# Deep transformer stack in one kernel: norms by column halves, a three-step root, one conditioning product and the side loads moved

## The chip, the cores and the metric

The kernel runs on one core of one Trainium2 chip. The metric is device time in microseconds (us) of one execution, as the median of several; less is better.

## What is computed

Two residual stacks, one after the other, all in 32-bit floats, with 256 tokens of width 1024. The first has two layers, each with four layer norms; the second has two layers with root-mean-square norms that are modulated by a conditioning vector, and mixtures of 16 experts. Cut to what matters here:

```python
for i in range(2):                                   # first block
    x = layer_norm(a * x + 0.5 * swiglu_ffn(x, ...), ...)            # FFN 0, FFN 2
    h = diff_attention(x) if i == 0 else pool_mixer(x)
    x = layer_norm(a * x + h, ...)                                   # mix_norm
    x = layer_norm(a * x + memory_cross_attention(x, mem, ...), ...) # xa_norm
    x = layer_norm(a * x + 0.5 * swiglu_ffn(x, ...), ...)            # FFN 1, FFN 3
for layer in range(2):                               # second block, lat = x
    mod_l = split(silu(c) @ ada_w[layer] + ada_b[layer], 6)          # and mod_c for the context
    h_l = rms_norm(lat, norm1_w) * (1 + mod_l[1]) + mod_l[0]
    y_l = hyena_mixer(h_l) if layer == 0 else sliding_window_attention(h_c, h_l)
    lat = lat + mod_l[2] * y_l
    h_l = rms_norm(lat, norm2_w) * (1 + mod_l[4]) + mod_l[3]
    lat = lat + mod_l[5] * expert_choice_ffn(h_l, ...)               # layer 0: the context too
return rms_norm(lat, final_norm_w)
```

## The kernel before

It is written out by hand, one instruction stream for each engine, with semaphores between them. The 256 tokens are NT = 2 tiles of 128 partitions; in the second block the context adds two more (tiles 2 and 3). A class `Plan` counts, in the order of the work, how many ring loads, work tiles, norms and parameter rows each stage uses, and every engine waits for counts worked out from it, so the order in the plan, in SP's loads and in TensorE's products has to be the same.

**The ring.** All weights pass through 12 slots of 1 MB (`ring`), loaded by SP in order. `load` (L707) waits until the slot's last user is done (`loads_used`). In the stages that use split weights (the four FFNs, the attention projections and outputs of the first block) a weight takes two slots, one for the value and one for its high part: VectorE or ScalarE rounds it, VectorE subtracts (`split_load` L2184, and L2191 and L2193 in the trace; `weight_low` L2200), and TensorE makes three products in place of one. `split_first` makes the first splits of an FFN early: in `cross_attention(1)` of VectorE (L2472) it stands behind ctx_norm and ahead of xa_norm1, and splits the first load of FFN 3.

**Work tiles and accumulators.** `work` is four banks that are used in turn; TensorE's `open_tile` waits until the bank's last content has been read. `acc` is four banks for one product of 256 x 1024: two column halves for each of two tiles.

**Norms.** `layer_norm` (L2290) waits for the tile's product, adds it to the rows (L2300), takes statistics (L2306), waits for ScalarE's square root, refines its reciprocal in five small steps (`newton_root` L2216), and writes the rows (L2319). It takes a gain row (L2312) and a bias row from `prow`. `mod_norm` (L2330) is the modulated one; `add_product` (L2660) adds the scaled product ahead of it. TensorE then turns the rows to columns (`normed_to_cols`, transposes, L875), and ScalarE copies them to SBUF (L1746 or, where it makes high parts, L1763).

**Parameter rows.** POOL loads gains, biases and modulation rows in a fixed order into the five slots of `prow` (L3029), each when an older row has been given back (`give_back`, L2396). Rows 14 to 16 belong to ctx_norm, rows 17 and 18 are the gain and bias of xa_norm1.

**Conditioning products.** `ada(q)`, q from 0 to 5, is 8 loads of 1 MB and 32 products of a 128 x 32 weight with 512 columns. ScalarE copies the result (`ada_out`), and POOL's `store_mods(q)` adds the bias (L3041), stores four rows to memory (L3045), waits for them and loads the next bias (L3033). ada(2) is done between values(1,1) and cross_attention(1), behind which stand ctx_norm, xa_norm1 and FFN 3. On TensorE, from L1654:

```python
            memory_values(1, 1)
            ada(2)
            cross_attention(1)
            normed_to_cols("ctx_norm", rows_h)
            normed_to_cols("xa_norm1", read=False)
            ffn(3)
```

On SP, L796 to L799, the loads are in the same order. On POOL, L3079 to L3088: rows up to 13, `store_mods(2)`, rows 14 to 16, then, once the last attention tile has been read, the load of the context, then rows 17 and on.

**Start.** ScalarE's queue loads the constants and x; POOL's queue, once x has landed (L3053 to L3064): mem (1 MB), three hyena tables, the router's weights, small vectors, the first conditioning bias, a mask and the first four parameter rows.

**First expert norm.** `moe_norm0` works on four tiles: lat (0, 1), whose product is hy_out0, and context (2, 3), whose product is hy_out1. For each pair VectorE mixes both tiles and then norms both. TensorE turns tiles 0 and 1 within hy_out1, then runs ada(3), then turns tiles 2 and 3. The loads of ada(3) are followed in the ring by those of expert 0.

Of the kernel before, what the change touches and what calls it, by code (L numbers as in the profile page):

```python
# [40 lines left out]
P = 128  # L41
# [191 lines left out]
def make_plan():  # L233
# [216 lines left out]
def build_program(nc, io, out, mod_rows, x_rows):  # L450
    plan = make_plan()
    with ExitStack() as ctx:
# [34 lines left out]
        head_tmp = sb("head_tmp", [P, NT * DA_H])  # L487
# [218 lines left out]
        def _(sp):  # L706
# [89 lines left out]
            load_values(1, 1)  # L796
            load_ada(2)
            load_cross_attention(1)
# [54 lines left out]
        def _(pe):  # L853
# [60 lines left out]
            def tile_to_acc(stage, n, x, j, last, blocks=range(KB)):  # L914
# [4 lines left out]
                for cb in range(2):  # L919
                    for half in range(2):  # L920
                        landed(n + 2 * cb + half)
                        w = slot(n + 2 * cb + half, 4)
                        for k in range(4):
                            kk = 4 * half + k
                            if kk not in blocks:
# [3 lines left out]
                               acc_full if fin and cb == 1 else None, done=int(last and k == 3))  # L929
# [66 lines left out]
            def out_product_split(stage, x_stage):  # L996
# [4 lines left out]
                for j in range(NT):  # L1001
# [3 lines left out]
                    for cb in range(2):  # L1005
                        for wp, xp in SPLIT_ORDER:
# [5 lines left out]
                            for half in range(2):  # L1012
# [6 lines left out]
                                for k in range(4):  # L1019
# [3 lines left out]
                                       kk == 0 and not wp and not xp, fin, acc_full if fin and cb == 1 else None,  # L1023
# [20 lines left out]
            def ffn(i):  # L1044
# [9 lines left out]
                def down(u, n, first_tile, tmore, smore, last=False):  # L1054
# [9 lines left out]
                    for h, j in order:  # L1064
                        for half in range(2):
                            final = last and h == 1 and half == 1
                            b, c = (2 * u + h) % 4, slice(half * 512, half * 512 + 512)
                            mm_split(acc[:, 2 * j + half, :],
                                     (gated_high[:, b, j * P:(j + 1) * P], gated_low[:, b, j * P:(j + 1) * P]),
                                     (high[:, h, c], low[:, h, c]), u == 0 and h == 0, last and h == 1,  # L1070
                                     acc_full if final else None, done=2 * int(h == 1 and j == NT - 1 and half == 1))
# [546 lines left out]
            pe.wait_ge(hy_landed, 16 * 3)  # L1618
            t = plan["hy_mlp1"].tiles
# [27 lines left out]
            for j in range(NT):  # L1647
                for g in range(4):
                    for a in range(2):
                        fin = g == 3 and a == 1  # L1650
                        mm(acc[:, 2 * j + g // 2, (g % 2) * 256:(g % 2) * 256 + 256],
                           pooled[:, 2 * g + a, j * P:(j + 1) * P], w[:, 2 * g + a, :], a == 0, a == 1,
                           acc_full if fin else None, done=int(fin and j == NT - 1))
# [84 lines left out]
        def _(act):  # L1738
# [241 lines left out]
            nc.scalar.activation(head_sq[:, 1, :], head_sq[:, 0, :], ACT.Sqrt).then_inc(root_ready, 1)  # L1980
# [38 lines left out]
            ada_out(2)  # L2019
# [112 lines left out]
            for s in range(2):  # L2132

                for i in range(NT * s, NT * (s + 1)):
                    norm_root("moe_norm0", i, i)
                if s:
                    ada_out(3)
                for i in range(NT * s, NT * (s + 1)):
                    cols_from_rows(col_tile("moe_norm0", i, 0), i * P)
# [25 lines left out]
        def _(dve):  # L2165
# [50 lines left out]
            def newton_root(v, s, r, tmp):  # L2216
# [975 lines left out]
```

## Time and profile before

| | |
|---|---|
| time, median of 3 runs | 2728.52 us (2727.0 to 2732.47) |
| the profiled execution's own time | 2730.94 us |
| its span, first to last instruction | 2728.9 us |
| TensorE (PE) busy | 2488.3 us, 91% |
| VectorE (DVE) busy | 1454.5 us, 53% |
| ScalarE (ACT) busy | 497.9 us, 18% |
| GpSimd (POOL) busy | 122.1 us, 4% |
| mean granted clock of TensorE | 0.96 |
| moved by DMA | 712.30 MB, mean 261 GB/s |

The page divides the span into 40 slices of 68 us. TensorE is busy for nine tenths or more in nearly all of them up to slice 30; the GB/s are between 58 and 280 up to slice 22 and about 422 in the two expert stages, where the chain that ended last runs through the loads ring<-in_moe_up and ring<-in_moe_down. PE is TensorE's matmul, PEld its weight load. A row of the timeline gives start, length, engine, source line, operation, output<-input, and in brackets how long the engine was idle before and what it waited for. SPq, ACTq and POOLq are DMA issues.

### The profile page before, as it was taken

The numbers are of one execution on the slowest core, as the hardware profiler recorded it, in microseconds if no ns is written. First come the engines' busy times: TensorE is split into PE (matmuls) and PEld (weight loads), VectorE is DVE, ScalarE is ACT, GpSimd is POOL, SyncE is SP. The second block draws the span as 40 slices with busy tenths as digits, with TensorE's granted clock in tenths as the row PEclk, the third lists the DMA queues.
The fourth block names the chain that finished last, engine by engine and source line by source line (L and its number), as shares of the span: only waits on it lengthen the run. The fifth ranks groups of instructions, "written<-read, shape, count | busy, mean of one in ns | idle before, by whom it ended". The sixth has DMA issues, their size and how long they took to land. (4 is left out here: it accounts for less than half of the span.)

```text
span 2728.9 us, 37076 instructions
## 1 busy us (share of the span) xinstructions
PE 2488.3 (91%) x14566; PEld 1708.9 (63%) x14566; DVE 1454.5 (53%) x2390; ACT 497.9 (18%) x942; POOL 122.1 (4%) x134
## 2 busy tenths in 40 slices
PE   7999999999999998998999799999999987777777
PEld 6997777999899588997676333333334863333333
DVE  6768554876876568767888623222234442112113
ACT  0004424100100131003331111111110631111111
POOL 1000000000000000003221100000000000000000
PEclk9999999999999998998999889999999998888898
DMA  7557642555556655561224899999996437999997
GB/s 252 185 215 280 245 147 93 182 185 200 170 186 212 251 172 179 185 204 58 62 62 162 336 398 422 422 422 422 422 420 263 171 115 324 422 422 422 422 422 308
DMA packets 234146, 712.30 MB, mean 261 GB/s; under 512 B 12645, under 2 KB 134517, under 8 KB 178624
## 3 DMA queue, kind: packets, MB, share of 16 engines
q1 hardware_dynamic: 223328, 676.37, 64.4%
q0 software_dynamic: 9856, 32.16, 3.3%
q10 hardware_dynamic: 864, 2.40, 0.2%
q8 instruction: 68, 1.11, 0.2%
q14 instruction: 30, 0.25, 0.0%
HBM read 708.69 MB, written 2.20 MB: 261 GB/s over the span
## 5 line engine op out<-in xcount | busy, mean ns | idle before, releaser
L859 PE MATMUL work<-ring,scratch 128*64 128x512 f32 (+1 forms) x3008 | 551.7, 636 | 107.6 <-DMA ring<-in_moe_up 69.8
L859 PE MATMUL work<-rows_h_parts,ring_parts 128*128 128x256 f32 x3072 | 550.5, 285 | 20.0 <-DVE ring_parts L2193 10.6
L859 PEld LDWEIGHTS work<-rows_h_parts,ring_parts 128*128 128x128 f32 x3072 | 477.1, 194 | 24.5 <-issue 10.3
L859 PEld LDWEIGHTS work<-ring,scratch 128*64 128x64 f32 (+1 forms) x3008 | 145.9, 126 | 489.0 <-issue 283.4
L859 PE MATMUL work<-cols_x_parts,ring_parts 128*128 128x256 f32 x1536 | 414.3, 285 | 0.0
L2193 DVE TENSOR_TENSOR ring_parts<-ring,ring_parts 128x2048 fp32r<-128x2048 f32 x132 | 302.6, 2292 | 4.5
L859 PEld LDWEIGHTS work<-cols_x_parts,ring_parts 128*128 128x128 f32 x1536 | 287.2, 194 | 1.5
L859 PE MATMUL acc<-ring_parts,rows_h_parts 128*128 128x512 f32 x896 | 264.3, 391 | 0.0
L2751 DVE COPY scratch<-work 128x512 f32<-128x512 f32 x32 | 22.1, 692 | 367.6 <-PE work L859 367.6
L859 PE MATMUL work<-scratch 128*128 128x256 f32 (+4 forms) x1040 | 198.8, 379 | 6.5 <-issue 4.2
L859 PEld LDWEIGHTS acc<-ring_parts,rows_h_parts 128*128 128x128 f32 x896 | 165.1, 188 | 33.2 <-issue 1.0
L2191 DVE CAST ring_parts<-ring 128x2048 fp32r<-128x2048 f32 x132 | 161.2, 1221 | 44.3 <-DMA ring<-in_ffn_w_in 36.0
L859 PEld LDWEIGHTS work<-scratch 128*128 128x128 f32 (+1 forms) x1040 | 151.8, 194 | 26.3 <-issue 12.4
L1785 ACT ACTIVATE scratch<-work 128x256 f32<-128x256 f32 x88 | 33.8, 384 | 674.4 <-PE work L859 674.4
L2761 DVE TENSOR_TENSOR scratch<-work,scratch 128x512 f32<-128x512 f32 x32 | 22.1, 692 | 229.9 <-PE work L859 229.9
L859 PE MATMUL acc<-ring_parts,scratch_parts 128*128 128x512 f32 x352 | 136.9, 389 | 0.0
L1889 ACT ACTIVATE scratch<-work 128x512 f32<-128x512 f32 x64 | 38.2, 597 | 496.9 <-PE work L875 275.7
L859 PE MATMUL work<-ring,cols_x 128*128 128x512 f32 x256 | 113.4, 604 | 1.9 <-ACT cols_x L1746 1.9
L2244 DVE TENSOR_TENSOR scratch<-scratch,work 128x256 f32<-128x256 f32 x88 | 37.0, 420 | 146.1 <-ACT scratch L1785 146.1
L2767 DVE TENSOR_TENSOR rows_x<-rows_x,work 128x512 f32<-128x512 f32 x128 | 83.7, 685 | 56.2 <-PE work L859 56.2
L859 PEld LDWEIGHTS work<-ring,cols_x 128*128 128x128 f32 x256 | 49.4, 194 | 63.2 <-issue 63.0
L1746 ACT ACTIVATE scratch<-work 128x512 f32<-128x512 f32 (+3 forms) x118 | 59.9, 524 | 156.9 <-PE work L859 110.2
(309 smaller groups left out, 2934.6 us busy)
## 6 DMA issues: line engine op xcount, KB each, us to landing
ring<-in_moe_down SPq DMA_DIRECT2D x128, 1024.0 KB, 25.9
ring<-in_moe_up SPq DMA_DIRECT2D x127, 1024.0 KB, 26.4
ring<-in_moe_gate SPq DMA_DIRECT2D x121, 1024.0 KB, 25.1
ring<-in_ffn_w_in SPq DMA_DIRECT2D x88, 1024.0 KB, 6.6
ring<-in_ada_w SPq DMA_DIRECT2D x48, 1024.0 KB, 11.6
ring<-in_ffn_w_out SPq DMA_DIRECT2D x44, 1024.0 KB, 6.3
ring<-in_xa_wkv SPq DMA_DIRECT2D x16, 1024.0 KB, 6.8
ring<-in_da_w_qkv SPq DMA_DIRECT2D x12, 1024.0 KB, 6.5
```

The source lines that it names most:

```text
L859: ins = nc.tensor.matmul(o, lhsT, rhs, start=start, stop=stop, **kw)
L1746: nc.scalar.activation(dst, src, ACT.Copy).then_inc(tile_read[t % 4], 1)
L1785: nc.scalar.activation(silu_buf[:, (2 * what[0] + what[1]) % 4, :], work[:, t % 4, 0:S], ACT.Silu).then_inc(silu_ready, 1)
L1889: nc.scalar.activation(dst, src, ACT.Copy).then_inc(tile_read[(t + q) % 4], 1)
L2191: nc.vector.tensor_copy(high, w).then_inc(arrived, 16)
L2193: nc.vector.tensor_tensor(low, w, high.bitcast(F32), ALU.subtract).then_inc(split_ready, 1)
L2244: step(nc.vector.tensor_tensor(g, silu_buf[:, m % 4, :], work[:, t % 4, S:2 * S], ALU.mult))
L2751: nc.vector.tensor_copy(up_part, work[:, b % 4, :]).then_inc(tile_read[b % 4], 1)
L2761: nc.vector.tensor_tensor(down_part, work[:, b % 4, :], out_gate, ALU.mult).then_inc(tile_read[b % 4], 1)
L2767: nc.vector.tensor_tensor(there, there, work[:, b % 4, :], ALU.add).then_inc(tile_read[b % 4], 1)
```

## The change

- **Side loads.** On POOL five small tables come first (positions, the two lambda vectors, the sub-norm gain, the sink). Then POOL waits for the sixth SiLU of FFN 0 before it loads mem, the hyena tables, the router, the bias, the mask and the rows.
- **Halves.** TensorE signals `acc_full` for each column half; the last FFN step goes half by half. `layer_norm` adds and takes statistics by halves, `add_product` multiplies and adds by halves.
- **Root.** ScalarE takes the root of four times the variance; VectorE needs three steps, not five. The head norm of the first attention has as many steps as before.
- **Conditioning product ada(2)** goes from ahead of mix_norm1 to between ctx_norm and xa_norm1, with its loads and its store.
- **First expert norm.** The context tiles are mixed and normed one after the other; TensorE runs ada(3) between turning tile 2 and tile 3.

```diff
-    norm("mix_norm1", before=[values(1, 1), ada(2)])
+    norm("mix_norm1", before=[values(1, 1)])
     cross_attention(1)
     norm("ctx_norm")
-    norm("xa_norm1")
+    norm("xa_norm1", before=[ada(2)])
...
-        if j == NT:
+        if j == NT + 1:
             ada(3)()
...
             load_values(1, 1)
+            load_cross_attention(1)
             load_ada(2)
-            load_cross_attention(1)
             ffn(3)
...
-                                       kk == 0 and not wp and not xp, fin, acc_full if fin and cb == 1 else None,
+                                       kk == 0 and not wp and not xp, fin, acc_full if fin else None,
...
-                    order = [(h, j) for h in range(2) for j in range(NT)]
+                    order = [(h, j, half) for h in range(2) for j in range(NT) for half in range(2)]
                     if last:
-                        order = [(h, j) for j in range(NT) for h in range(2)]
+                        order = [(h, j, half) for j in range(NT) for half in range(2) for h in range(2)]
...
             memory_values(1, 1)
-            ada(2)
             cross_attention(1)
             normed_to_cols("ctx_norm", rows_h)
+            ada(2)
             normed_to_cols("xa_norm1", read=False)
             ffn(3)
...
+            normed_to_cols("moe_norm0", rows_h, tiles=[NT], read=False)
             ada(3)
-            normed_to_cols("moe_norm0", rows_h, tiles=range(NT, 2 * NT))
+            normed_to_cols("moe_norm0", rows_h, tiles=[NT + 1])
+            for piece in range(2):
+                read_out(pe, col_tile("moe_norm0", NT, piece))
...
-                nc.scalar.activation(root[:, i:i + 1], spread[:, i:i + 1], ACT.Sqrt).then_inc(root_ready, 1)
+                nc.scalar.activation(root[:, i:i + 1], spread[:, i:i + 1], ACT.Sqrt, scale=-1.0).then_inc(root_ready, 1)
...
             memory_values(1, 1)
-            ada_out(2)
             cross_attention(1)
             for j in range(NT):
                 norm_root("ctx_norm", j, NT + j)
             norm_root("xa_norm1", 0, 0)
             for j in range(NT):
                 cols_from_rows(col_tile("ctx_norm", j, 0), (NT + j) * P)
-            split_cols("xa_norm1", 0)
+            ada_out(2)
             norm_root("xa_norm1", 1, 1)
-            split_cols("xa_norm1", 1)
+            for j in range(NT):
+                split_cols("xa_norm1", j)
...
-                step(nc.vector.reciprocal(r, s))
-                step.settle()
-                step(nc.vector.tensor_tensor(tmp, r, r, ALU.mult))
-                step.settle()
-                step(nc.vector.tensor_tensor(tmp, tmp, v, ALU.mult))
-                step.settle()
-                step(nc.vector.tensor_scalar(tmp, tmp, -0.5, 1.5, ALU.mult, ALU.add))
-                step.settle()
-                step(nc.vector.tensor_tensor(r, r, tmp, ALU.mult))
+            def newton_root(minus_four, half, r):
+
+
+                step(nc.vector.reciprocal(half, half))
+                step.settle()
+                step(nc.vector.scalar_tensor_tensor(out=r, in0=half, scalar=half, in1=minus_four, op0=ALU.mult, op1=ALU.mult))
+                step.settle()
+                step(nc.vector.scalar_tensor_tensor(out=r, in0=r, scalar=3.0, in1=half, op0=ALU.add, op1=ALU.mult))
                 step.settle()
...
                     for h in range(2):
-                        step(nc.vector.bn_stats(stats[:, j, h, :], rows_x[:, j, h * 512:(h + 1) * 512]))
+                        half = rows_x[:, j, h * 512:(h + 1) * 512]
+                        if prepare is None:
+
+                            dve.wait_ge(acc_full, 2 * (NT * use + j) + h + 1)
+                            ins = nc.vector.scalar_tensor_tensor(out=half, in0=half, scalar=x_scale, in1=acc[:, 2 * j + h, :],
+                                                                 op0=ALU.mult, op1=ALU.add)
+                            if h:
+                                ins.then_inc(acc_read, 1)
+                                dve.wait_ge(acc_read, NT * use + j + 1)
+                            else:
+                                step(ins)
+                                step.settle()
+                        step(nc.vector.bn_stats(stats[:, j, h, :], half))
...
                     if not last:
-
+                        if free is not None and i >= NT:
+                            dve.wait_ge(acc_full, 2 * NT * (plan[free].acc + 1))
                         step(nc.vector.tensor_tensor(h, x, factor, ALU.mult))
...
-                    if out_bias:
+                    mix_first = out_bias and s != streams[-1]
+                    if mix_first:
 
                         for i in mine:
                             mix(i, scale)
                         give_back(2)
                     for i in mine:
-                        if mix is not None and not out_bias:
+                        if mix is not None and not mix_first:
                             mix(i, scale)
...
+            pool.wait_ge(silu_ready, plan["ffn0"].silu + 2 * FFN_HEAD)
             pool.dma_start(rows_x[:, NT:2 * NT, :], io["mem"][0].rearrange("(j p) d -> p j d", p=P)).then_inc(mem_landed, 16)
...
             before_ctx = 8 * DEPTH - 2
-            rows_until(before_ctx)
-            store_mods(2)
             rows_until(before_ctx + 3)
 
             at = plan["xa_att1"]
             read_out(pool, at.tiles + attention_order(NT * XA_H)["o", NT * XA_H - 1])
             pool.dma_start(rows_x[:, NT:2 * NT, :], io["ctx"][0].rearrange("(j p) d -> p j d", p=P)).then_inc(ctx_landed, 16)
-
-
+            store_mods(2)
             rows_until(before_ctx + 10)
```

## Rows read from the trace of the kernel before

**Rows 1.** The page: busy time of the engines; GB/s in 40 slices of 68 us.
```profile
PE 2488.3 (91%) x14566; PEld 1708.9 (63%) x14566; DVE 1454.5 (53%) x2390; ACT 497.9 (18%) x942; POOL 122.1 (4%) x134
...
GB/s 252 185 215 280 245 147 93 182 185 200 170 186 212 251 172 179 185 204 58 62 62 162 336 398 422 422 422 422 422 420 263 171 115 324 422 422 422 422 422 308
```

**Rows 2.** Waits, 0 to 80 us: us in total, times, longest.
```profile
PE work L859 <- DVE ring_parts L2193: 9.4, 3, 7.5
```

**Rows 3.** Timeline, VectorE's fourth weight split: start, us.
```profile
36.19 1.23 DVE L2191 CAST ring_parts<-ring 128x2048 fp32r<-128x2048 f32 x1 [5.99 <-DMA ring<-in_ffn_w_in]
```

**Rows 4.** Windows: length, busy by engine, granted clock, DMA share, GB/s.
```profile
39.80:44.00 4.20, 4.20 (x19) 4.20 (x20) 4.10 (x5) 0.00 (x0) 0.00 (x0) 0.50 0.95 344
...
48.00:52.00 4.00, 4.00 (x30) 3.74 (x29) 3.90 (x5) 0.39 (x1) 0.00 (x0) 1.00 0.02 4
```

**Rows 5.** DMA queues, 0 to 100 us: POOL's queue, packets, MB, share.
```profile
q0 software_dynamic: 1344, 4.27, 12.9%
```

**Rows 6.** Timeline, ffn_norm0: add, statistics, root's first step, output, TensorE's wait.
```profile
211.81 1.28 DVE L2300 SCALAR_TENSOR_TENSOR rows_x<-rows_x,acc 128x512 f32<-128x512 f32 x2 [2.93 <-PE acc L859]
213.13 1.29 DVE L2306 BATCH_NORM_STATS2 stats<-rows_x 128x6 f32<-128x512 f32 x2
...
215.96 0.16 DVE L2218 RECIPROCAL rstd<-root 128x1 f32<-128x1 f32 x1
...
216.92 1.28 DVE L2319 SCALAR_TENSOR_TENSOR rows_x<-rows_x,rstd,prow 128x1024 f32<-128x1024 f32 x1
...
226.53 2.13 PE L875 MATMUL work<-consts,rows_x 128*128 128x128 f32 x16 [3.14 <-DVE cols_x_parts L2213]
```

**Rows 7.** Timeline, ada(2): its products, ScalarE's copy, the next parameter row.
```profile
942.26 7.07 PE L859 MATMUL work<-ring,act_col 128*32 128x512 f32 x64
...
949.46 0.60 ACT L1746 ACTIVATE ada_raw<-work 128x512 f32<-128x512 f32 x1 [6.50 <-PE work L859]
...
958.93 0.54 POOL L3029 DMA_DIRECT2D prow<-in_norm_w  x1
```

**Rows 8.** Timeline around ctx_norm and xa_norm1.
```profile
997.75 0.55 POOL L3029 DMA_DIRECT2D prow<-in_ln_g  x1 [0.33 <-issue]
...
1013.21 1.27 SPq L719 DMA_DIRECT2D ring<-in_ffn_w_in  x2
...
1016.64 1.23 DVE L2191 CAST ring_parts<-ring 128x2048 fp32r<-128x2048 f32 x1
...
1019.37 1.91 PE L875 MATMUL work<-consts,rows_h 128*128 128x128 f32 x16
...
1020.12 1.28 DVE L2300 SCALAR_TENSOR_TENSOR rows_x<-rows_x,acc 128x512 f32<-128x512 f32 x2
...
1023.29 2.04 ACT L1746 ACTIVATE cols_x<-work 128x512 f32<-128x512 f32 x4
...
1032.98 1.97 PE L875 MATMUL work<-consts,rows_x 128*128 128x128 f32 x8 [4.29 <-DVE rows_x L2319]
```

**Rows 9.** Timeline, eight products of ada(4) after a wait.
```profile
2044.69 1.94 PE L859 MATMUL work<-ring,act_col 128*32 128x512 f32 x8 [1.42 <-DMA ring<-in_ada_w]
```

**Rows 10.** DMA issues, 706 to 709 us: a parameter row, KB, us to landing.
```profile
prow<-in_pool_scale POOLq DMA_DIRECT2D x1, 512.0 KB, 4.3
```

**Rows 11.** Timeline, the last tile of mod_norm0 turned.
```profile
1247.30 1.97 PE L875 MATMUL work<-consts,rows_h 128*128 128x128 f32 x8 [3.57 <-DVE rows_h L2357]
```

**Rows 12.** Timeline: ada(3), last tile of moe_norm0; the window of the DMA gap.
```profile
1540.21 5.36 PE L859 MATMUL work<-ring,act_col 128*32 128x512 f32 x48
...
1554.56 1.97 PE L875 MATMUL work<-consts,rows_h 128*128 128x128 f32 x8 [5.03 <-DVE rows_h L2357]
...
1582.00:1584.00 2.00, 2.00 (x8) 0.64 (x6) 0.00 (x0) 0.00 (x0) 0.00 (x0) 0.57 0.46 70
```

**Rows 13.** Timeline: the last tile of moe_norm1 turned; the program's last output rows.
```profile
2246.83 1.97 PE L875 MATMUL work<-consts,scratch 128*128 128x128 f32 x8 [7.00 <-DVE scratch L2357]
...
2724.57 1.28 DVE L2354 SCALAR_TENSOR_TENSOR rows_h<-rows_x,rstd,prow 128x1024 f32<-128x1024 f32 x1
```

More of the change, by code:

```diff
@@ L928, in tile_to_acc @@
                             mm(acc[:, 2 * j + cb, :], x(kk, j), w[:, k, :], kk == 0, fin,
-                               acc_full if fin and cb == 1 else None, done=int(last and k == 3))
+                               acc_full if fin else None, done=int(last and k == 3))
             def split_done(stage, k):
@@ L1060, in down @@
                     high, low = parts(n, 2)
-                    order = [(h, j) for h in range(2) for j in range(NT)]
+                    order = [(h, j, half) for h in range(2) for j in range(NT) for half in range(2)]
                     if last:
-                        order = [(h, j) for j in range(NT) for h in range(2)]
[L1064 to L1071, printed above, removed]
+                        order = [(h, j, half) for j in range(NT) for half in range(2) for h in range(2)]
+                    for h, j, half in order:
+                        final = last and h == 1
+                        b, c = (2 * u + h) % 4, slice(half * 512, half * 512 + 512)
+                        mm_split(acc[:, 2 * j + half, :],
+                                 (gated_high[:, b, j * P:(j + 1) * P], gated_low[:, b, j * P:(j + 1) * P]),
+                                 (high[:, h, c], low[:, h, c]), u == 0 and h == 0, final,
+                                 acc_full if final else None, done=2 * int(h == 1 and j == NT - 1 and half == 1))
                 def run(events, tb, lb, it, tper, lper):
@@ L2131, in _ @@
                     hyena_highs(c + 2, 0)
[L2132 to L2139, printed above, removed]
+            for i in range(NT):
+                norm_root("moe_norm0", i, i)
+            for i in range(NT):
+                cols_from_rows(col_tile("moe_norm0", i, 0), i * P)
+            norm_root("moe_norm0", NT, NT)
+            cols_from_rows(col_tile("moe_norm0", NT, 0), NT * P)
+            norm_root("moe_norm0", NT + 1, NT + 1)
+            ada_out(3)
+            cols_from_rows(col_tile("moe_norm0", NT + 1, 0), (NT + 1) * P)
             experts(0)
@@ L2327, in tile_root, with mod_norm @@
                 c = slice(i, i + 1)
-                newton_root(spread[:, c], root[:, c], rstd[:, c], newton[:, c])
-            def mod_norm(stage, streams, mix=None, out_bias=False, last=False, dst=lambda i: rows_h[:, i, :]):
+                newton_root(spread[:, c], root[:, c], rstd[:, c])
+            def mod_norm(stage, streams, mix=None, out_bias=False, last=False, dst=lambda i: rows_h[:, i, :], free=None):
                 at = plan[stage]
@@ L2390, in mod_norm @@
                         norm_tile(i, factor, shift)
-                    give_back(2 * int(not last) + 1 + int(mix is not None and not out_bias))
+                    give_back(2 * int(not last) + 1 + int(mix is not None and not mix_first) * (1 + int(out_bias)))
             def give_back(rows):
@@ L2663, in mix @@
                     at, j = plan[name(i // NT)], i % NT
[L2664 removed]
                     step.settle()
[L2666 to L2669 removed]
+                    for h in range(2):
+                        c = slice(h * 512, h * 512 + 512)
+                        dve.wait_ge(acc_full, 2 * (NT * at.acc + j) + h + 1)
+                        ins = nc.vector.tensor_tensor(mix_tmp[:, c], acc[:, 2 * j + h, :], scale[:, c], ALU.mult)
+                        if h:
+                            ins.then_inc(acc_read, 1)
+                            dve.wait_ge(acc_read, NT * at.acc + j + 1)
+                        else:
+                            step(ins)
+                            step.settle()
+                        step(nc.vector.tensor_tensor(rows_x[:, i, c], rows_x[:, i, c], mix_tmp[:, c], ALU.add))
                     step.settle()
@@ L2943, in _ @@
             dve.wait_ge(x_back, 32)
[L2944 removed]
+            mod_norm("moe_norm0", [0, 1], mix=add_product(lambda s: f"hy_out{s}"), out_bias=True, free="hy_out1",
                      dst=lambda i: h_main[:, i, :] if i < NT else rows_h[:, i, :])
```

60 lines of the change are left out of this document (27 added, 33 removed).

## The prediction

> **What bounds the kernel now.** I read the page first. TensorE is busy for 91% of the span, and the line of GB/s is flat at about 422 in slices 24 to 30 and 34 to 38 [rows 1]. So there are two kinds of stage: up to slice 22 TensorE sets the pace and an edit is worth what it takes out of TensorE's idle time; in the two expert stages the transfers do, and an edit is worth what it moves the point from which they run without a gap. Next I read what TensorE waited for in the first 80 us, then the timeline of each norm that the diff touches, and for each moved step the timelines of SP and POOL, whose queues run in order.
>
> **Start of the kernel.** TensorE loses 9.4 us to weight splits, 7.5 of them at once [rows 2]. VectorE makes these splits and was itself waiting for the load that it splits, 6.0 us at 36.19 [rows 3]. Then TensorE runs at 0.50 of its clock, that is at 1.2 of its 2.4 GHz, from 39.80 to 44.00 [rows 4]. In the same time POOL's queue moves 4.27 MB [rows 5]: mem, tables and parameter rows. The change lets all but the five small ones wait for the sixth SiLU of the first FFN. Removed: the two later stalls, 8.8 us, and half of 4.2 us at the low clock, 2.1; together 11.0 us (bounds 8 and 12). The first stall, 0.6, is VectorE's own and stays. The delayed transfers then land beside FFN 0; cover for them is there, since the DMA engines move only 4 GB/s in 48 to 52 while TensorE is busy all the time [rows 4]. Cost 0.
>
> The Trainium skill, "DMA: Bandwidth & Descriptors", section "Issuing engines are not separate DMA queues", speaks against this edit: transfers issued by any engine share the same 16 DMA engines and interleave. By it the bytes are only moved and can delay ring loads later; by the row of 48 to 52 there is idle time to take them. The first would make the sum some 10 us longer, and that is one of the rivals below.
>
> **Halves and the three-step root.** Each norm tile has five small steps of the root, from 215.96 to 216.92, 0.96 us, so 0.19 each [rows 6]; two less save 0.385 per tile. Where VectorE waits for the accumulator, as at 211.81 [rows 6], the first half (0.64 for the add, 0.65 for its statistics [rows 6]) can be done before the second half of the product is there: 1.25 us, once per norm, less 0.04 for a settle in each tile. The variance still takes two steps, so nothing there. What counts is whether TensorE waits:
> - ffn_norm0: TensorE waits 3.14 us at 226.53 for VectorE [rows 6]. 1.25 + 2 x 0.385 - 0.05 = 2.0 gained (at most 3.1).
> - mix_norm0, xa_norm0, ffn_norm1, ffn_norm2: in none did I find TensorE waiting for the rows; key and value products lie over them. 0, and if that cover were gone 0.8 to 2.0 each to be had.
> - mod_norm0 with ffn_norm3 ahead of it: four tiles in a chain, TensorE waits 3.57 us for the last [rows 11]. 1.25 + 4 x 0.385 - 0.1 = 2.7 gained.
> - moe_norm1: TensorE waits 7.00 us [rows 13]; the add and statistics of the first half lie under the product, the root is shorter: 2.0 gained, and the expert stage starts that much earlier.
> - mod_norm1 0.4 and last_norm 2 x 0.385 = 0.8 (VectorE's chain ends the program, last tile at 2724.57 [rows 13]).
> The head norm of the first attention has as many steps as before: 0.
>
> **First expert norm tile by tile.** Tile 2 is now normed before tile 3 is mixed, but its output may be written only once hy_out1 is done, so it comes some 3.5 us after 1540.21, and only then does TensorE run ada(3), which before began at 1540.21 [rows 12]. TensorE turns the last tile some 2 us sooner than 1554.56 [rows 12]. But the loads of expert 0 wait in the ring for ada(3)'s slots, and from there on the DMA engines are all but saturated until their one gap around 1582 (0.46 of their share in 1582 to 1584 [rows 12]). Starting them 4 to 5 us later fills that gap and then costs something; the two mixes by halves add 0.8 before. I take 1.0 lost, between 2.5 gained and 4 lost.
>
> **Conditioning product ada(2).** Here the sign is decided. Removed: 7.0 us of TensorE at 942.26 [rows 7], bare, since the mix norm needs only values(1,1) as cover (its second tile is ready then). So everything up to xa_norm1 is 7.0 earlier. All times below are the old ones less 7.0. Three queues are passed:
> 1. SP. The eight ada(2) loads now stand behind xa_out1 and ahead of ffn(3). Ring of 12 slots: the last four ada(2) loads need the first four slots of xa_out1, freed where SP issued at 1013.21 [rows 8], now 1006.2; the first load of ffn(3) needs the fifth of them, freed as the second block of the last tile ends (1011.6), and queues behind four ada loads. Five loads of 1 MB at about 2.5 us (422 GB/s [rows 1]) plus 2 for the start: it lands at 1021.3. Before, it had landed long ago, and VectorE split it at 1016.64 with no wait [rows 8]. VectorE's order is ctx_norm, this split, xa_norm1. It comes to the split at 1008.9 (two roots shorter) and waits 12.4 us. Split 3.5 (1016.64 to 1020.12), so xa_norm1 starts at 1024.8.
> 2. ScalarE reads the ctx tiles only after the root of xa_norm1's tile 0, 3.2 us after that norm starts (1020.12 to 1023.29 [rows 8]): 1028.0, and for 2.0 us. TensorE, done with the ctx turns at 1014.4 (the time of [rows 8] less 7.0), waits for these reads. ada(2) starts at 1030.1. After so long an idle time it starts at the low clock, where eight of its products take 1.94 us [rows 9] instead of 0.88 (7.07/8 [rows 7]): about 2 more, so it ends at 1039.2.
> 3. POOL. store_mods(2) now stands behind the ctx load and ahead of the parameter rows 17 and 18. Those are ln_g and ln_b of xa_norm1, which went out right behind the ctx load at 997.75 [rows 8]. Row 17 now needs ScalarE's copy of ada(2), the sum, four stores, their landing, and the bias load: 9.5 us from 949.46 to 958.93 [rows 7]. So it goes out at 1048.8 and lands 4.3 to 7 us later (4.3 with little else in flight [rows 10]; I take 4.5, as the ring is full by then): 1053.3. VectorE stands in xa_norm1's tile 0 with the variance done, waiting for the gain row. Then 1.28 + 0.58 + 1.28: tile 0 at 1056.5; tile 1 is 6.1 later (6.4 before, from 1020.12 and 1032.98), 1062.6.
> TensorE turned that tile at 1032.98 [rows 8]. So 29.6 us are lost here, with the 7.0 already credited; bounds 25 and 34, from the landings (4.3 to 7; 5 loads at 2.5 to 3) and the low clock.
>
> **Sum.** -11.0 - 2.0 + 29.6 - 2.7 + 1.0 - 0.4 - 2.0 - 0.8 = +11.7. The profiled execution took 2730.94 us (span 2728.9), the median is 2728.52; the sum gives 2742.6 against the first and 2740.2 against the second. I predict 2740.2.
>
> **Rivals.**
> - The change does what it is meant to do: neither row nor load is late. For it speaks that the bare waits for xa_norm1 and TensorE's 7.0 us are real; against it the order of two queues. Tile 1 is then turned at 1025.9, 36.7 us better: 2703.5.
> - Only the ring load is late, the row is in time (if rows 17 and 18 went out before the store). Tile 1 at 1040.3: 2717.9.
> - Only the row is late, the load in time: ada(2) ends at 1025.3, row at 1039.4, tile 1 at 1048.6: 2726.2, no change that counts.
> - Slower still: the 4.1 MB of side loads meet the ring loads of FFN 0 and delay a split beyond its lead. It decides from the point where a ring load lands more than one FFN half later than now; the price is the DMA time of these bytes, 4.1 MB at 400 GB/s, 10 us, and all the start gained is given back: 2750.
>
> **How the numbers follow.** Forecast 0.62, with a range of its own of 2734 to 2746 from the bounds at the start, at xa_norm1 and at the expert stage. Slower still 0.09, row only 0.08, load only 0.08, neither 0.08, between these 0.05. About 0.2%, 5.5 us, is what a measurement of this kernel tells from no change. Faster by more: neither, load only and a little: 0.18. Within: row only and the forecast's tail: 0.11. Slower: 0.71. For 8 in 10 I take in row only and slower still: 2725 to 2751.
>
> **What the new profile would show.** No split stall of TensorE near 40 us, and the second FFN step about 11 us sooner. In the waits: VectorE idle 10 to 14 us for ring<-in_ffn_w_in just before xa_norm1 and about 24 us for the ln_g row inside its first tile, TensorE idle some 15 us before ada(2) and again after it. mix_norm1 is followed at once by the turns. ada(3) starts about 5 us after hy_out1, and the DMA gap near 1582 is gone. The prediction is wrong if the ln_g row does not wait for the store of ada(2), or if ffn(3)'s first load comes before ada(2)'s.

## The result, and the profile after

The changed kernel takes 2743.72 us (median of 4 runs, 2742.9 to 2746.08) against 2727.76 us for the kernel before; the ratio is 1.0053 (95% interval 1.0041 to 1.0065), so it is slower by 11 to 18 us. The prediction was 2740.2 us, 11.7 more than before. The profiled execution has a span of 2743.4 us against 2728.9: 14.5 more.

The page after: busy time of the engines, and GB/s in 40 slices, to be read against [rows 1].

```profile
PE 2486.0 (91%) x14566; PEld 1698.2 (62%) x14566; DVE 1449.1 (53%) x2337; ACT 497.3 (18%) x942; POOL 123.3 (4%) x134
...
GB/s 244 237 236 292 178 146 111 193 184 211 157 184 243 140 172 162 185 206 100 62 62 161 265 419 422 422 422 422 422 422 291 170 92 328 422 422 422 422 422 312
```

The work of the engines has hardly changed: TensorE has 2.3 us less, VectorE 5.4 less, POOL 1.2 more. The time is in waits, and the waits of 1000 to 1070 us say which (us in total, times, longest):

```profile
DVE rows_x L2320 <- DMA prow<-in_ln_g: 28.4, 1, 28.4
...
PE work L874 <- DVE rows_x L2325: 24.0, 2, 19.7
...
PE work L858 <- ACT cols_x L1748: 16.7, 1, 16.7
...
DVE ring_parts L2194 <- DMA ring<-in_ffn_w_in: 12.7, 1, 12.7
```

In the kernel before, the same stretch has no wait for a row or for a load. The timeline shows the waits of the changed kernel in their order (start, us, engine, line; in brackets the idle time before it and what ended it):

```profile
998.52 25.05 SPq L718 DMA_DIRECT2D ring<-in_ffn_w_in  x4
...
1008.63 1.23 DVE L2194 CAST ring_parts<-ring 128x2048 fp32r<-128x2048 f32 x1 [12.74 <-DMA ring<-in_ffn_w_in]
...
1012.10 0.68 DVE L2303 SCALAR_TENSOR_TENSOR rows_x<-rows_x,acc 128x512 f32<-128x512 f32 x1
...
1015.40 2.04 ACT L1748 ACTIVATE cols_x<-work 128x512 f32<-128x512 f32 x4
1017.80 9.65 PE L858 MATMUL work<-ring,act_col 128*32 128x512 f32 x64 [16.66 <-ACT cols_x L1748]
...
1027.57 0.60 ACT L1748 ACTIVATE ada_raw<-work 128x512 f32<-128x512 f32 x1 [10.13 <-PE work L858]
...
1036.94 0.54 POOL L3051 DMA_DIRECT2D prow<-in_ln_g  x1 [0.49 <-issue]
...
1043.68 1.28 DVE L2320 SCALAR_TENSOR_TENSOR rows_x<-rows_x,mean_var,prow 128x1024 f32<-128x1024 f32 x1 [28.43 <-DMA prow<-in_ln_g]
...
1053.40 1.97 PE L874 MATMUL work<-consts,rows_x 128*128 128x128 f32 x8 [4.26 <-DVE rows_x L2325]
```

The reader sees one chain through five engines. VectorE comes out of ctx_norm at 995.9 and stands 12.7 us in front of the split of a load that SP could issue only behind the eight of ada(2). Its statistics of xa_norm1 come late by that, ScalarE's root and reads of the ctx tiles behind them, TensorE's ada(2) behind those, ScalarE's copy behind ada(2), POOL's store behind the copy, and the row ln_g behind the store. For that row VectorE stands another 28.4 us inside tile 0. In [rows 8] the same split ran with no wait and the last tile was turned at 1032.98.

How far the changed kernel is from the one before at the same instruction, from both timelines:

| TensorE at | before | after | difference | step |
|---|---|---|---|---|
| first turn of ffn_norm0 | 221.43 | 210.75 | -10.7 | start -10.7 |
| its last turn | 226.53 | 213.28 | -13.3 | ffn_norm0 -2.6 |
| last turn of xa_norm1 | 1032.98 | 1053.40 | +20.4 | ada(2) +33.7 |
| last turn of mod_norm0 | 1247.30 | 1265.11 | +17.8 | -2.6 |
| last turn of mod_norm1 | 2054.09 | 2069.81 | +15.7 | moe_norm0, experts 0, mod_norm1 -2.1 |
| last turn of moe_norm1 | 2246.83 | 2261.27 | +14.4 | -1.3 |
| VectorE's last output row | 2724.57 | 2739.03 | +14.5 | last norm 0.0 |

### The profile page after: what moved, and what is told of

Its sections match the earlier page's. It is cut to its first block and busy times, and to the rows that moved or that the text cites. A ratio compares the mean times of both kernels' runs of the same rounds, so it can differ in the third digit from the quotient of the medians.

```text
span 2743.4 us, 37025 instructions
## 1 busy us (share of the span) xinstructions
PE 2486.0 (91%) x14566; PEld 1698.2 (62%) x14566; DVE 1449.1 (53%) x2337; ACT 497.3 (18%) x942; POOL 123.3 (4%) x134
## 5 line engine op out<-in xcount | busy, mean ns | idle before, releaser
L858 PE MATMUL work<-ring,scratch 128*64 128x512 f32 (+1 forms) x3008 | 557.5, 642 | 111.1 <-DMA ring<-in_moe_up 69.9
L858 PEld LDWEIGHTS work<-rows_h_parts,ring_parts 128*128 128x128 f32 x3072 | 475.2, 193 | 15.9 <-issue 9.9
L858 PEld LDWEIGHTS work<-scratch 128*128 128x128 f32 (+1 forms) x1040 | 148.6, 191 | 25.1 <-issue 12.4
```

The source lines that it names most:

```text
L858: ins = nc.tensor.matmul(o, lhsT, rhs, start=start, stop=stop, **kw)
```

## The experiments

Each was timed beside the kernel before. The last column is the ratio's distance from 1 times 2730 us; its interval is about 2.5 to 4 us to either side. Times at an instruction are from the one profiled execution of each kernel, and such an execution can lie 2 us or more from the median.

| run | median us | ratio to before (95%) | us against before |
|---|---|---|---|
| changed kernel | 2743.72 | 1.0053 (1.0041 to 1.0065) | +14.5 |
| row_first | 2720.27 | 0.9961 (0.9947 to 0.9974) | -10.6 |
| split_behind | 2729.06 | 0.9995 (0.9986 to 1.0004) | -1.4 |
| both_moved | 2704.80 | 0.9902 (0.9887 to 0.9917) | -26.8 |
| ada_back | 2710.84 | 0.9928 (0.9914 to 0.9941) | -19.7 |
| only_ada | 2761.49 | 1.0114 (1.0099 to 1.0129) | +31.1 |
| only_start | 2719.02 | 0.9960 (0.9947 to 0.9972) | -10.9 |
| only_math | 2719.34 | 0.9962 (0.9949 to 0.9975) | -10.4 |
| ctx_reads_first | 2732.24 | 1.0012 (1.0003 to 1.0021) | +3.3 |
| copy_first | 2730.76 | 1.0002 (0.9993 to 1.0010) | +0.5 |
| moe_back | 2741.47 | 1.0046 (1.0034 to 1.0058) | +12.6 |
| both_root | 2701.97 | 0.9895 (0.9881 to 0.9909) | -28.7 |
| both_root_moe_back | 2703.24 | 0.9904 (0.9890 to 0.9918) | -26.2 |

**Is the whole loss in the move of ada(2)?** The move undone on all five queues, the rest kept (ada_back), and the move alone on the kernel before (only_ada). The edit of ada_back on the plan, SP and POOL; TensorE's and ScalarE's parts go back in the same way:

```diff
-    norm("mix_norm1", before=[values(1, 1)])
+    norm("mix_norm1", before=[values(1, 1), ada(2)])
...
-    norm("xa_norm1", before=[ada(2)])
+    norm("xa_norm1")
...
-            load_cross_attention(1)
             load_ada(2)
+            load_cross_attention(1)
...
-            rows_until(before_ctx + 3)
+            rows_until(before_ctx)
+            store_mods(2)
+            rows_until(before_ctx + 3)
```

> The changed kernel with the conditioning product ada(2) put back to its old place on all five queues, its loads and store_mods(2) with it; all else as changed. Theory (the whole loss is in this move, net of the 7.1 us that it takes from the mix norm): the second tile of xa_norm1 is turned 13.2 us earlier than in the kernel before, 33.7 earlier than in the changed kernel, so 33 us less than the changed kernel, about 19 less than the kernel before. Rival (a part of the loss comes from the side loads, which now meet the ring loads of the first FFN, or from the norms' new order): clearly less than 33, below 25.

> The kernel before with one part of the change alone: the conditioning product ada(2) moved to xa_norm1, on SP, TensorE, ScalarE and POOL. Theory: the whole loss of the change is here; the product's 7.1 us at the mix norm are gained and about 40.5 are lost at xa_norm1, so 33 us more than the kernel before. Rival (the loss needs the other parts, which make everything ahead of xa_norm1 earlier and so the ring load relatively later): 25 or less.

ada_back is at -19.7 us, so 34.2 less than the changed kernel; only_ada is at +31.1. Both are what the theory gave (-19 and +33), and both are beyond the 25 at which the rivals began, only_ada's interval too (27 to 35). What the change loses, it loses by this move. Only_ada's waits of 1000 to 1070 us show the same two late transfers with none of the other edits in the kernel:

```profile
DVE rows_x L2314 <- DMA prow<-in_ln_g: 27.0, 1, 27.0
...
PE work L859 <- ACT cols_x L1746: 16.6, 1, 16.6
...
DVE ring_parts L2191 <- DMA ring<-in_ffn_w_in: 12.3, 1, 12.3
```

**Which of the two comes last?** Row_first repairs the row alone, split_behind the load alone, both_moved both.

```diff
+            rows_until(before_ctx + 5)
             store_mods(2)
             rows_until(before_ctx + 10)
```

```diff
-                split_first(2 * i + 1, 1)
+                if i == 0:
+                    split_first(2 * i + 1, 1)
                 layer_norm(f"xa_norm{i}", f"xa_out{i}", ALPHA, LN_EPS)
```

> The changed kernel with one step of POOL's queue moved: the parameter rows 17 and 18 (ln_g and ln_b of xa_norm1) go out right behind the ctx load and ahead of store_mods(2), as they did before the change. Theory (two late things, of which the row comes last): the rows land near 1005 us, long before they are wanted; VectorE still begins xa_norm1 at 1012.1, since the load of ffn(3) is as late as ever; ada(2) still runs from 1017.8 to 1027.5 and is now what comes last. The second tile is turned near 1029.5 instead of 1053.4: 24 us less than the changed kernel, about 9.5 less than the kernel before. Rival 1 (the row is late for another cause, such as its slot in the ring of rows): no change. Rival 2 (only the ring load decides): no change, and only the split's place helps.

> The changed kernel with VectorE's split of the first load of ffn(3) taken from ahead of xa_norm1 and made behind it; POOL's queue stays as changed. Theory: xa_norm1 begins at once behind ctx_norm, at 995.9 instead of 1012.1, so ScalarE reads the ctx tiles 16 us earlier and ada(2) runs from about 1002 to 1011.5; the row still waits for the store behind it (9.5 us) and its landing (6.7), is there near 1027.5 instead of 1043.7, and the second tile is turned near 1037: 16 us less than the changed kernel, so about 1.5 less than the kernel before. Rival (the ring load itself is what ada(2) or the row waits for): the late load then holds the same things as before, and no more than 4 us are gained.

> Both repairs at once: rows 17 and 18 ahead of store_mods(2), and the split of ffn(3)'s first load behind xa_norm1; ada(2) stays under the norm, where the change put it. Theory: nothing of xa_norm1 waits for a transfer; its second tile is done near 1008.6, ada(2) ends near 1011.5, the late load lands near 1008.6 and is split by 1012, and ffn(3) begins about 40 us earlier than in the changed kernel (1056.1): about 40 us less than the changed kernel, 25 less than the kernel before. Rival (the two waits hide a third of the same length, such as the second load of ffn(3), which queues behind the same transfers): 5 to 15 us of this stay in new waits of TensorE for splits at the start of ffn(3).

Against the changed kernel they gain 25.1, 15.9 and 41.3 us, where 24, 16 and 40 were expected. Each rival falls: the row is held by the store and nothing else, and the load matters although the row comes last, because ada(2), on which the row waits, hangs on it. The timeline of row_first shows the load as late as ever and ada(2) 0.5 us later, with no wait for a row; the tile is now turned at 1031.8, not at the 1029.5 expected, since VectorE waits 5.70 us for a root that stands behind the copy of ada(2):

```profile
1009.17 1.23 DVE L2194 CAST ring_parts<-ring 128x2048 fp32r<-128x2048 f32 x1 [12.87 <-DMA ring<-in_ffn_w_in]
...
1018.34 9.73 PE L858 MATMUL work<-ring,act_col 128*32 128x512 f32 x64 [16.78 <-ACT cols_x L1748]
...
1031.79 1.09 PE L874 MATMUL work<-consts,rows_x 128*128 128x128 f32 x8 [2.69 <-DVE rows_x L2325]
```

So at the tile row_first is 21.6 us ahead of the changed kernel, where 24 was expected. Another 3.3 us come between mod_norm0 and mod_norm1, a stretch that varies from run to run (see below); that the medians give 25.1 is in part luck.

In split_behind ada(2) starts 15 us sooner and at full clock, and the row is still the last thing to come:

```profile
1002.69 7.07 PE L858 MATMUL work<-ring,act_col 128*32 128x512 f32 x64 [1.15 <-ACT cols_x L1748]
...
1020.25 0.54 POOL L3052 DMA_DIRECT2D prow<-in_ln_g  x1 [0.49 <-issue]
1026.48 1.28 DVE L2320 SCALAR_TENSOR_TENSOR rows_x<-rows_x,mean_var,prow 128x1024 f32<-128x1024 f32 x1 [26.96 <-DMA prow<-in_ln_g]
```

**Is it one chain or two losses?** If it is one chain, the load must be to be had off it without touching the split. The reads of the ctx tiles go ahead of the root of tile 0 (ctx_reads_first), and then the copy of ada(2) too (copy_first):

```diff
-            norm_root("xa_norm1", 0, 0)
             for j in range(NT):
                 cols_from_rows(col_tile("ctx_norm", j, 0), (NT + j) * P)
             ada_out(2)
+            norm_root("xa_norm1", 0, 0)
```

That is copy_first; in ctx_reads_first the root stands between the reads and ada_out(2).

> The changed kernel with one step of ScalarE moved: its reads of the ctx tiles stand ahead of the root of xa_norm1's first tile instead of behind it. The late load and the late row stay. Theory (the chain to the row runs load, split, statistics, root, ctx reads, ada(2), store, row; this takes ada(2) off the load): ada(2) runs from about 1002 instead of 1017.8, the row is there near 1027.5 instead of 1043.7, and 16 us are gained against the changed kernel, as much as by the split behind the norm, although xa_norm1 itself still begins at 1012. Rival (the load and the row are two separate losses that add up): the row's part stays, under 5 gained.

> The last edit on ScalarE one instruction further: the ctx reads and also its copy of ada(2) stand ahead of the root of xa_norm1's first tile. In the run before, ada(2) itself ran from 1002.8 to 1009.9, but its copy waited until 1015.9 behind that root, which waits for the late split. Theory: the copy is made at 1010, the row goes out near 1020 instead of 1025.9 and is there near 1026.5; 5 us less than that run, 16 to 17 less than the changed kernel, 1.5 to 2 less than the kernel before. Rival (the copy is not what POOL's queue waits for): no gain over that run.

Ctx_reads_first gains 11.2 us against the changed kernel, not 16. The expectation had overlooked the copy: ada(2) was done at 1009.9, but its copy stood in ScalarE's queue behind a root that waits for the late split.

```profile
1002.80 7.07 PE L858 MATMUL work<-ring,act_col 128*32 128x512 f32 x64 [1.15 <-ACT cols_x L1748]
...
1015.79 0.20 ACT L1799 ACTIVATE root<-spread 128x1 f32<-128x1 f32 x1 [13.36 <-DVE spread L2315]
1015.90 0.58 ACT L1748 ACTIVATE ada_raw<-work 128x512 f32<-128x512 f32 x1
```

With the copy ahead as well, it is made at 1008.73, the row goes out at 1021.11 instead of 1025.86, and xa_norm1's last tile is turned at 1036.99, 16.4 us sooner than in the changed kernel. The medians give 14.0 us, with an interval that holds both 14 and 16. It is one chain: the late load costs time through the row. That the gains of the two repairs add up all the same (25.1 and 15.9 against 41.3 together) is no contradiction, as each repair takes one link out of a series.

**What is left between the two repairs and more?** In both_moved VectorE waited 3.65 us for a root that stood behind the copy of ada(2). The split behind the norm has a price too, which the theory of both_moved left out and its rival put at 5 to 15 us: it stands ahead of VectorE's split columns of the last tile (L2216), for which TensorE now waits:

```profile
PE work L858 <- DVE cols_x_parts L2216: 3.6, 1, 3.6
```

ffn(3) starts 4.69 us after the last turn in both_moved and in split_behind, and 2.70 us after it in the changed kernel: 2.0 us lost. The edit of both_root moves the root alone:

```diff
-            ada_out(2)
             norm_root("xa_norm1", 1, 1)
+            ada_out(2)
```

> The kernel with both repairs, and ScalarE's root of xa_norm1's second tile ahead of its copy of ada(2) instead of behind it. In the run with both repairs VectorE waited 3.65 us for this root, TensorE 2.68 for the tile's rows and 3.60 for its split columns. Theory: these waits are one chain and shrink by the 3.6 together: 3 us less than both_moved, about 28 less than the kernel before. Rival (the late ring load is what is left): under 1 us less.

It is at -28.7 us, as expected, though 1.9 from both_moved lies within the intervals. By the profiled executions ffn(3) starts at 1013.07 instead of 1018.72 (1.2 us of that is there before xa_norm1), and VectorE's last output row is 4.2 us earlier than in both_moved. This is the lowest median measured: ada(2) under xa_norm1 is then worth having, some 9 us more than ada_back.

**The other parts.** The start alone (the POOL part of the diff and its three waits, on the kernel before), and the halves with the root alone (the changed kernel less the side loads, the move of ada(2) and the new order of the first expert norm).

> The kernel before with the start alone: mem, the tables and the parameter rows wait on POOL for the sixth SiLU of the first FFN. Theory: the split stalls near 40 us and the low clock behind them go, and nothing is given back later: 10.7 us less than the kernel before, from the first turned tile of ffn_norm0 to the end. Rival (the same bytes land beside FFN 0 and delay ring loads): between 0 and 5 less. A third: the gain is lost again in the expert stages, where the transfers set the pace, because the ring cannot run further ahead there: under 8 less.

> The kernel before with the norms by column halves and the three-step root alone (no moved transfers, no moved conditioning product, the first expert norm in its old order, though its mixes go by halves). Theory: 2.6 at ffn_norm0, 2.6 at ffn_norm3 and mod_norm0, about 1.4 at moe_norm1 and 0.5 at the last norm: 7 us less than the kernel before. Rival (the halves help where no wait was seen, at the other norms too): 10 or more. Rival (the settles between the halves cost as much as they bring): under 3.

Only_start is at -10.9 us, so within its interval (7.6 to 14.5) the 11.0 is kept to the end. Only_math is at -10.4, where 7 was expected and the first rival began at 10; its interval, 6.8 to 13.9 us, holds both. By the profiled executions the difference to before is, in us:

| last turn of | ffn_norm0 | xa_norm1 | mod_norm0 | mod_norm1 | moe_norm1 | end |
|---|---|---|---|---|---|---|
| only_start | -11.2 | -9.3 | -9.2 | -14.0 | -12.9 | -12.9 |
| only_math | -2.5 | -3.4 | -5.9 | -10.4 | -11.8 | -12.4 |

In both, 4.5 us or more come between mod_norm0 and mod_norm1, where the first expert stage lies, and the 7 expected had nothing there. But these are not shown to be the norms' work: only_start has the norms of the kernel before and gains 4.9 there. This stretch took from 801.4 to 806.4 us in the eight runs whose code in it is the changed kernel's (that kernel itself: 804.7), and from 801.9 to 806.8 in the three whose code in it is the old one (before: 806.8, only_ada 803.3, only_start 801.9). It varies by 5 us with no edit in it, and before's profiled execution is the longest of all. One part of the spread is the clock: ahead of mod_norm1 the last two groups of ada(4) ran at the full clock in only_math, 1.06 us each, while in the kernel before ([rows 9]) and in the changed one they took 1.94:

```profile
2036.29 1.06 PE L858 MATMUL work<-ring,act_col 128*32 128x512 f32 x8 [1.42 <-DMA ring<-in_ada_w]
2038.78 1.06 PE L858 MATMUL work<-ring,act_col 128*32 128x512 f32 x8 [1.43 <-DMA ring<-in_ada_w]
```

The group behind the first waits for its load either way, so of the 1.8 only the last group's 0.9 can count. What makes up the rest of the spread, no run takes apart.

**The first expert norm tile by tile.** Put back to the old order, in the changed kernel (moe_back) and in the best one (both_root_moe_back):

```diff
-            normed_to_cols("moe_norm0", rows_h, tiles=[NT], read=False)
             ada(3)
-            normed_to_cols("moe_norm0", rows_h, tiles=[NT + 1])
-            for piece in range(2):
-                read_out(pe, col_tile("moe_norm0", NT, piece))
+            normed_to_cols("moe_norm0", rows_h, tiles=range(NT, 2 * NT))
```

> The changed kernel with the first expert norm in its old order: both second-stream tiles mixed first, ada(3) between hy_out1 and the turns, its copy behind both roots; all else as changed. The prediction had the new order cost 1.0 us; the trace of the changed kernel shows it 1.2 us nearer to the kernel before between mod_norm0 and the end of the first expert stage. Theory (the stage behind is paced by transfers, and all that counts is when they run without a gap): the two differ by less than 2 us, and the old order is 1 us slower. Rival (the later ada(3) starves the ring of expert 0): the old order is 3 to 5 us faster.

> The last kernel with the first expert norm in its old order. It asks the same as moe_back at another phase of the ring. Theory: within 2 us of the last kernel, 1 us slower. Rival (the new order starves the ring): 3 to 5 us faster.

The old order is 1.9 us faster in the one pair and 2.5 slower in the other, by the ratios; the intervals overlap in both. The expectation "within 2 us, the old order 1 slower" is neither shown nor refuted. The profiled executions are shorter with the old order in both pairs: from mod_norm0's last turn to mod_norm1's, moe_back gains 5.3 us on the kernel before and the changed kernel 2.1; in the other pair it is 6.4 and 3.4. These 3 us are less than the 5 by which this stretch varies with its code unchanged, so they decide nothing. What the profile does show is what the new order does. Windows of 10 us of the changed kernel and then of moe_back (length, busy by engine, granted clock, DMA share, GB/s):

```profile
1560.00:1570.00 10.00, 8.71 (x64) 2.87 (x68) 8.80 (x16) 1.29 (x3) 0.00 (x0) 0.83 0.75 279
1570.00:1580.00 10.00, 4.98 (x93) 3.19 (x85) 2.79 (x12) 3.77 (x7) 3.27 (x5) 0.97 1.01 419
```

```profile
1560.00:1570.00 10.00, 5.83 (x56) 2.06 (x48) 9.54 (x20) 1.87 (x5) 2.31 (x3) 1.00 0.93 366
```

With the new order ada(3) starts at 1562.31 instead of 1557.73, and the transfers stand longer for its slots: in 1560 to 1570 they move less by (366 - 279) x 10 / 422 = 2.1 us of transfer time. TensorE makes the 64x64 turn behind the gate at 1584.30 instead of 1586.45 in exchange; behind it the transfers set the pace, not TensorE.

## Why the prediction was right, and where a size was off

**The sign and the mechanism** were right, step by step. The prediction's times at xa_norm1 are the old ones less 7.0, and leave out what the start and ffn_norm0 had gained by then. Moved by those 13.25 us (226.53 less 213.28), they stand against the trace:

| step at xa_norm1 | predicted | measured | off by |
|---|---|---|---|
| ffn(3)'s first load is there | 1008.05 | 1008.63 | 0.6 |
| xa_norm1 starts | 1011.55 | 1012.10 | 0.6 |
| ada(2) starts | 1016.85 | 1017.80 | 1.0 |
| ada(2) ends | 1025.95 | 1027.45 | 1.5 |
| row 17 goes out | 1035.55 | 1036.94 | 1.4 |
| VectorE has it | 1040.05 | 1043.68 | 3.6 |
| tile 1 is turned | 1049.35 | 1053.40 | 4.1 |

Two steps of the sum don't add up as written: five loads at 2.5 us and 2 more from 1006.2 give 1020.7 and not 1021.3, so the load came 1.2 us later than the terms say, and 8.8 and 2.1 at the start are 10.9, not 11.0. The 4.27 MB of [rows 5] are those of the first 100 us, not of the low clock's 4 us alone.

**The term that was mis-sized** is this one: +29.6 was +33.7, within its bounds of 25 to 34. Half of the 4.1 is the landing of the row: 6.7 us from issue (1036.94 to 1043.68), where 4.5 was taken out of 4.3 to 7. The ring was full by then, as said; what the reason left out are the four rows that go out right behind row 17, 0.5 us apart. In the DMA queues of 1037 to 1044 us (packets, MB, share) POOL's is all but alone, with one packet of another beside it:

```profile
q0 software_dynamic: 414, 1.51, 82.3%
```

So five rows are in flight within 2.2 us of the first. [rows 10], the row from which 4.3 was taken, had one other row beside it: POOL's queue moved 1.05 MB in 706 to 712 us there. That the rows behind it delay the first is argued, not shown, since no run sends it alone at this place; with the same five rows it landed after 5.6 to 6.2 us in only_ada, split_behind, ctx_reads_first and copy_first. Another 0.6 is ada(2) at 9.65 instead of 9.1 us: after 16.7 us of idle time it began at the low clock, and did not reach the full one at once.

**The start:** -11.0 forecast, -10.7 in the trace, -10.9 in the run of its own. The page of the Trainium skill that spoke against it ("DMA: Bandwidth & Descriptors", section "Issuing engines are not separate DMA queues") says rightly that the bytes still share the 16 engines; what decided is that there was idle transfer time to take them. In the changed kernel 52 to 60 us moved 48 GB/s and 60 to 80 moved 384 (340 and 180 in the kernel before), with TensorE busy in all of both.

**Halves and root:** ffn_norm0 -2.0 forecast, -2.6 measured; mod_norm0 -2.7 and -2.6; moe_norm1 -2.0 and -1.3, as its tile was turned after 5.62 us of waiting instead of [rows 13]'s 7.00. The last norm -0.8 and 0.0 against the turn of moe_norm1: its two output rows stand 4.20 us apart instead of 4.48, so a tile saves 0.28, not 0.385, as two of the fused steps take 0.22 each where the single ones took 0.16. The 0.6 of the two tiles does not appear in the difference because the expert stage ahead of them was that much longer; it varies by as much between runs.

**First expert norm and experts 0:** +1.0 forecast with mod_norm1's -0.4, -2.1 measured for the three. The gap near 1582 is gone, as said, but it was not filled: it moved ahead to 1560 to 1570, where the loads wait for ada(3). The 2.7 us by which the prediction is off here stay unexplained: the stretch varies by 5 us with its code unchanged, and only_start gains 4.9 in it, so neither the 1.0 charged to the new order nor the 0.8 charged to the mixes by halves is tested by it.

**Errors of both signs:** +4.1 at xa_norm1, +0.8 at the last norm, +0.7 at moe_norm1, +0.3 at the start, -2.7 around experts 0, -0.6 at ffn_norm0 and +0.1 at mod_norm0 make the 2.7 by which 14.46 stands above 11.7, up to rounding. That the sum is so near is partly luck: the two largest errors have opposite signs. The four rivals were tested by name: "neither late" was put at 2703.5 (both_moved: 2704.80), "only the load" at 2717.9 (row_first: 2720.27), "only the row" at 2726.2 (split_behind: 2729.06). The fourth, side loads that delay FFN 0, falls with only_start.

## What to carry to other kernels

A product that only fills idle time has a queue on each engine that it touches. Moving it under another norm moves its loads ahead of the next stage's, its copy ahead of the norm's reads and its store ahead of the norm's parameter rows; list these for SP, ScalarE and POOL before looking at TensorE's gain. Here 7 us were gained and 41 lost, and with three steps put elsewhere the kernel is some 9 us faster than with the product in its old place. Where a transfer is late, look whether the instruction that waits for it must stand where it stands: the split taken behind the norm cost 2 us at the start of ffn(3) and gained 16 in all.

## What the runs showed of the hardware that was not expected

**POOL and VectorE held each other up.** POOL's add of 128x512 took 1.25 us in the changed kernel, with VectorE idle. In copy_first, issued 0.03 us after a two-operand VectorE instruction had begun, it took 3.38:

```profile
1009.44 2.29 DVE L2196 TENSOR_TENSOR ring_parts<-ring,ring_parts 128x2048 fp32r<-128x2048 f32 x1
```

```profile
1009.47 3.38 POOL L3063 TENSOR_TENSOR ada_sum<-ada_sum,ada_raw 128x512 f32<-128x512 f32 x1 [32.76 <-ACT ada_raw L1748]
```

2.2 us until VectorE's next instruction began (1011.65) and 1.25 of its own make 3.4; in both_root it was 3.31. In both_moved POOL came first, and VectorE's step of the root, 128x1, took 1.10 us instead of 0.22, ending when POOL's add did (row_first shows the same):

```profile
1011.19 1.26 POOL L3064 TENSOR_TENSOR ada_sum<-ada_sum,ada_raw 128x512 f32<-128x512 f32 x1 [31.66 <-ACT ada_raw L1748]
...
1011.36 1.10 DVE L2224 SCALAR_TENSOR_TENSOR rstd<-root,spread 128x1 f32<-128x1 f32 x1
```

The Trainium skill ("SBUF — State Buffer", section "SBUF: two separate sides") says that a VectorE operation with two SBUF inputs and a GpSimd operation that reads SBUF exclude each other for a whole instruction. These rows agree. In copy_first it put 2.1 us on the chain to the row, which went out 12.4 us after the start of the copy instead of 9.4; in the changed kernel the add met an idle VectorE.

**The clock.** The same 64 products of ada(2) took 7.07 us after 1.15 us of idle time and 9.65 after 16.66; after as long a wait they took 9.73 in row_first and 8.78 in only_ada. The windows of the changed kernel show the granted clock at 0.50 in 1018 to 1022 and 0.87 in 1022 to 1026, that is from 1.2 to 2.4 GHz within the product:

```profile
1018.00:1022.00 4.00, 4.00 (x20) 0.91 (x16) 0.00 (x0) 0.00 (x0) 0.00 (x0) 0.50 0.21 59
1022.00:1026.00 4.00, 4.00 (x40) 1.28 (x36) 0.00 (x0) 0.00 (x0) 0.00 (x0) 0.87 0.99 312
```
